# One Trainium2 core: the opening of a three-layer transformer kernel, rearranged

## What is computed

```python
h = jnp.concatenate([meta, x], axis=1)                  # 16 + 256 rows of 2048
xn = h * rsqrt(mean(h * h) + 1e-6) * g_pre_mix
proj = xn @ w_in                                        # the first 512 columns are S5's input u
a_bar = exp(lam * exp(log_dt))                          # 32 groups x 64 complex states
states = associative_scan(a_bar, u @ b_bar)             # s[t] = a_bar * s[t-1] + b_bar u[t]
y = real(c @ states) + d * u
```

## Time and profile before

| | us |
|---|---|
| median of 3 runs | 3298.6 |
| lowest, highest | 3298.03, 3300.4 |
| span of the profiled execution | 3298.9 |
| TensorE busy in it | 3269.3 |
| VectorE, ScalarE, GpSimd busy | 1971.1, 1513.7, 275.8 |

### The profile page before, as it was taken

The page is one execution under the profiler, slowest core; times in us unless marked ns, Lnnn a source line. Parts: engine busy times, 40 slices in busy tenths (PEclk is TensorE's granted clock), DMA queues, the critical chain, the costliest instruction groups (busy, mean ns, idle before and its releaser), DMA issues.

```text
span 3298.9 us, 45001 instructions
## 1 busy us (share of the span) xinstructions
PE 3269.3 (99%) x17255; PEld 2811.2 (85%) x17255; DVE 1971.1 (60%) x2228; ACT 1513.7 (46%) x1754; POOL 275.8 (8%) x238
## 2 busy tenths in 40 slices
PE   8999999999999999999999999999999999999999
PEld 7998888888888888888888888888888888888887
DVE  7888665555555655565555555564656555555565
ACT  5335454344444544545443444454454534444444
POOL 6432000000000034000000000001400000000000
PEclk9999999999999999999999999999999999999999
DMA  7544555655555555455555666655545565666664
GB/s 208 154 129 162 195 192 191 190 186 188 196 194 191 168 183 166 141 179 183 188 189 191 189 193 191 191 176 173 180 146 177 191 192 188 190 190 192 191 192 152
DMA packets 249097, 598.55 MB, mean 181 GB/s; under 512 B 22297, under 2 KB 63993, under 8 KB 247945
## 3 DMA queue, kind: packets, MB, share of 16 engines
q1 hardware_dynamic: 247800, 591.10, 56.2%
q0 software_dynamic: 800, 5.31, 0.4%
q10 hardware_dynamic: 384, 0.58, 0.1%
HBM read 594.86 MB, written 2.10 MB: 181 GB/s over the span
## 4 chain that ended last, share of the span: by engine, by line
PE 95%; DVE 3%; ACT 1%; DVEq 1%; issue 0%; DMA 0%; ACTq 0%; POOLq 0%
PE ps L1023 31%; PE ps L628 21%; PE ps L1281 19%; PE ps L634 11%; PE ps L984 3%; PE ps L706 2%; PE ps L698 2%; PE ps L699 1%; PE ps L571 1%; DVE wlo L2040 1%; PE ps L1171 0%; PE ps L1170 0%; PE ps L580 0%; DVE wlo L2647 0%; PE ps L1205 0%
## 5 line engine op out<-in xcount | busy, mean ns | idle before, releaser
L2040 DVE TENSOR_TENSOR wlo<-raw,whi 128x2048 fp32r<-128x2048 f32 (+1 forms) x425 | 973.6, 2291 | 653.3 <-ACT whi L1397 652.7
L1397 ACT CAST whi<-raw 128x2048 fp32r<-128x2048 f32 (+2 forms) x427 | 809.3, 1895 | 532.1 <-PE ps L634 426.0
L628 PE MATMUL ps<-xT,whi 128*128 128x512 f32 x3072 | 733.5, 391 | 1.4 <-DVE xT L2058 1.1
L1023 PE MATMUL ps<-whi,stage 128*128 128x512 f32 x3040 | 725.9, 389 | 0.0
L1023 PEld LDWEIGHTS ps<-whi,stage 128*128 128x128 f32 x3040 | 570.3, 188 | 118.1
L628 PEld LDWEIGHTS ps<-xT,whi 128*128 128x128 f32 x3072 | 564.6, 188 | 111.6 <-issue 1.3
L1281 PE MATMUL ps<-whi,xT 128*128 128x512 f32 (+1 forms) x1792 | 444.5, 389 | 1.1 <-DVE wlo L2647 0.9
L634 PEld LDWEIGHTS ps<-xT,wlo 128*128 128x128 f32 x3072 | 393.9, 191 | 15.0
L634 PE MATMUL ps<-xT,wlo 128*128 128x256 f32 x3072 | 398.5, 283 | 0.0
L1754 ACT CAST stage<-big 128x256 fp32r (+1 forms) x384 | 137.0, 404 | 546.4 <-PE ps L1023 535.5
L1023 PE MATMUL ps<-wlo,stage 128*128 128x512 f32 x1520 | 381.1, 389 | 0.0
(11 more groups left out here) (424 smaller groups left out, 2332.1 us busy)
## 6 DMA issues: line engine op xcount, KB each, us to landing
raw<-in_mlp_w SPq DMA_DIRECT2D x128, 1024.0 KB, 5.1
raw<-in_w_up SPq DMA_DIRECT2D x128, 1024.0 KB, 5.3
raw<-in_w_down SPq DMA_DIRECT2D x128, 1024.0 KB, 5.5
raw<-in_w_in SPq DMA_DIRECT2D x100, 1024.0 KB, 5.1
raw<-in_w_o SPq DMA_DIRECT2D x32, 1024.0 KB, 5.5
raw<-in_w_out SPq DMA_DIRECT2D x16, 1024.0 KB, 5.0
raw<-in_w_in SPq DMA_DIRECT2D x16, 832.0 KB, 4.4
raw<-in_w_uq SPq DMA_DIRECT2D x4, 1024.0 KB, 5.0
```

The lines of the kernel that those rows point to most:

```text
L628: mm(psum(bank + j), whi[:, u % 2, c:c + P], xT[:, k, :], start=k == 0, stop=False)
L1023: return mm(psum(bank + 2 * r + n), x_of(kk, part, r), w[:, u % 2, c:c + 512], start=begin and kk == part == 0 and w is whi, stop=stop)
L1397: act.copy(whi[:, u % 2, 0:width], raw[:, u, 0:width]).then_inc(sig["hi"], 1)
L2040: tt(wlo[:, u % 2, 0:width], raw[:, u, 0:width], whi[:, u % 2, 0:width].bitcast(F32), SUB).then_inc(sig["lo"], 1)
```

## The change

Four things, all in the first 60 us:

1. *Meta rows over 128 partitions.* Each meta row is loaded as 8 rows of 256 (`xm`, [128, 256]). VectorE squares them, TensorE sums the 8 parts by a mask matrix made from the identity (`meta_mask`), ScalarE and VectorE make the inverse root, GpSimd scales, TensorE turns two blocks, VectorE multiplies by the gains, ScalarE and VectorE write the high and the low part straight into `xT1`. A chain of nine steps on one semaphore, `meta`. The tiles' transposes and evictions have 256 columns now. The products still have 272.
2. *Squares shared, loads moved.* VectorE squares x's first half and half of the second, ScalarE the other half. The constants, the meta rows and the gain `g_pre_mix` are loaded by ScalarE's queue, the other eight small vectors by SP's, ahead of the weights. Fillers: 5, 4 and 5 instead of 12 and 12. The gain has a transpose of its own, early; the other vectors' transpose comes after tile 7.
3. *First panel cast in pieces and used by row tile.* ScalarE casts four pieces of 512, one after every two tiles; TensorE takes both column blocks of a tile as it comes (`both_high`), after tiles 0 to 7.
4. *S5 tables doubled together.* The angle times 16 is wrapped and put through the sines together with the angle (128 x 32 instead of 128 x 16), and both tables grow in one doubling of four rounds with twice the columns. The S5 steps on ScalarE and VectorE stand later: exponential after tile 15, `angles` and `first_power` after the low half of panel 1, the sines after the cast of panel 2, and `tiles(U_STAGE, 0)` behind them.

```diff
 tensor
-            pe.wait_ge(sig["ld_cst"], 16)
-            keep_busy(12, 1)
-            pe.wait_ge(sig["ld_rows"], 16 * N_ROW_LOADS)
-            pe.wait_ge(sig["dtr"], 1)
-            tr(psum(0, P), colrow[0], ident).then_inc(sig["cpy"], 1)
-            keep_busy(12, 1)
...
-                    tr(psum(4 + k % 4, META), xm[:, c], ident[0:META, 0:META])
                     for r in range(RT):
-                        last = tr(psum(4 + k % 4, P, at=META + P * r), x[:, r, c], ident)
+                        last = tr(psum(4 + k % 4, P, at=P * r), x[:, r, c], ident)
...
+            pe.wait_ge(sig["ld_cst"], 16)
+            keep_busy(5, 1)
+            pe.wait_ge(sig["meta"], M_SQUARED)
+            mm(psum(3, 1), meta_mask, ss[:, 2:3], start=True, stop=True).then_inc(sig["meta"], 1)
+            pe.wait_ge(sig["ld_g"], 16)
+            tr(psum(6, KD), colrow[0][0:KD, :], ident[0:KD, 0:KD]).then_inc(sig["gcl"], 1)
+            keep_busy(4, 1)
+            pe.wait_ge(sig["meta"], M_SCALED)
+            for j in range(2):
+                last = tr(psum(2, P, at=P * j), xm[:, P * j:P * j + P], ident)
+            last.then_inc(sig["meta"], 1)
+            keep_busy(5, 1)
+            pe.wait_ge(sig["xna"], 1)
             pe.wait_ge(sig["xn"], norm_at["xn"] + 1)
             rows_in(0, 4)
             pe.wait_ge(sig["xn"], norm_at["xn"] + 2)
             rows_in(4, 8)
-            pe.wait_ge(sig["cols"], 1)
+            pe.wait_ge(sig["ld_rows"], 16 * N_ROW_LOADS)
+            pe.wait_ge(sig["dtr"], 1)
+            tr(psum(3, P, at=SEQ), colrow[0], ident).then_inc(sig["cpy"], 1)
...
+                    def both_high():
+                        pe.wait_ge(sig["meta"], M_LOW)
+                        for k in range(8):
+                            if k < 6:
+                                pe.wait_ge(sig["hi0"], k // 2 + 1)
+                            else:
+                                pe.wait_ge(sig["hi"], 4 * (Q + q) + 1)
+                            pe.wait_ge(sig["xt"], norm_at["xt"] + k + 1)
+                            for j in range(2):
+                                hi = whi[:, 0, k * 256 + j * P:k * 256 + j * P + P]
+                                mm(psum(j, L), hi, xT1[:, k, 0, :], start=k == 0, stop=False)
+                                mm(psum(j, L), hi, xT1[:, k, 1, :], start=False, stop=False)
+                    if first and u == 0:
+                        both_high()
+                        pe.wait_ge(sig["xnp"], 1)
+                        pe.wait_ge(sig["xnh"], 1)
+                        rows_in(8, 12)
+                        low(0)
+                        rows_in(12, KD)
+                        low(1)
+                        continue
+                    if first and u == 1:
+                        high(0)
+                        high(1)
+                        low(0)
+                        low(1)
+                        continue
 scalar
-            fn(big[:, 0:D], x[:, 0, :], ACT.Square, accum_out=ss[:, 0:1])
...
+            act.wait_ge(sig["meta"], M_SUMMED)
+            fn(rs[:, 2:3], psum(3, 1), ACT.Sqrt, scale=1.0 / D, bias=eps).then_inc(sig["meta"], 1)
             act.wait_ge(sig["ld_x1"], 16)
+            fn(big[:, 3072:4096], x[:, 1, 0:1024], ACT.Square, accum_out=ss[:, 3:4])
+            act.wait_ge(sig["xsq"], 1)
+            fn(rs[:, 0:1], ss[:, 0:1], ACT.Sqrt, scale=1.0 / D, bias=eps)
             act.drain()
+            act.wait_ge(sig["xsq"], 2)
+            fn(rs[:, 1:2], ss[:, 3:4], ACT.Sqrt, scale=1.0 / D, bias=ss[:, 1:2]).then_inc(sig["ss"], 1)
+            act.wait_ge(sig["meta"], M_GAINED)
+            fn(xT1[:, :, 0, 0:META], meta_t.rearrange("p (k m) -> p k m", m=META), ACT.Copy).then_inc(sig["meta"], 1)
             act.wait_ge(sig["rsr"], first["rsr"] + 1)
+            fn(x[:, 1, 0:512], x[:, 1, 0:512], ACT.Copy, scale=rs[:, 1:2]).then_inc(sig["xna"], 1)
...
+            act.wait_ge(sig["raw0"], 16 * (Q + 1))
+            for i in range(4):
+                rows_hi(2 * i, 2 * i + 2)
+                c = slice(512 * i, 512 * i + 512)
+                act.copy(whi[:, 0, c], raw[:, 0, c]).then_inc(sig["hi0" if i < 3 else "hi"], 1)
+            rows_hi(8, 12)
+            split(Q, 1, D, used=False)
+            rows_hi(12, KD)
+            act.wait_ge(sig["cols"], 1)
+            fn(prm[:, 0, :], cols[:, V_LOG_DT:V_LOG_DT + ST], ACT.Exp).then_inc(sig["prm_a"], 1)
+            split(Q, 2, D)
+            act.wait_ge(sig["prm_b"], 1)
+            fn(prm[:, 7, :], prm[:, 1, :], ACT.Exp)
+            fn(ang[:, 3, :], ang[:, 1, :], ACT.Sin)
+            fn(ang[:, 4, :], ang[:, 2, :], ACT.Sin).then_inc(sig["prm_a"], 1)
+            tiles(U_STAGE, 0)
+            split(Q, 3, D)
 vector
+            dve.wait_ge(sig["ld_x"], 16)
+            stt(big[:, 0:D], x[:, 0, :], 1.0, x[:, 0, :], MUL, MUL, accum_out=ss[:, 0:1]).then_inc(sig["xsq"], 1)
+            dve.wait_ge(sig["meta"], M_ROOT)
+            dve.reciprocal(rs[:, 2:3], rs[:, 2:3]).then_inc(sig["meta"], 1)
+            dve.wait_ge(sig["ld_x1"], 16)
+            stt(big[:, D:D + 1024], x[:, 1, 1024:D], 1.0, x[:, 1, 1024:D], MUL, MUL, accum_out=ss[:, 1:2])
...
+            dve.wait_ge(sig["meta"], M_TURNED)
+            dve.drain()
+            tt(meta_t.rearrange("p (b j m) -> p b j m", b=8, j=2), psum(2, META_COLS).rearrange("p (j m b) -> p b j m", j=2, m=META),
+               cols[:, 0:KD].rearrange("p (b j) -> p b j", j=2).unsqueeze(3).to_broadcast([P, 8, 2, META]), MUL)\
+                .then_inc(sig["meta"], 1)
...
+            dve.wait_ge(sig["meta"], M_HIGH)
+            tt(xT1[:, :, 1, 0:META], meta_t.rearrange("p (k m) -> p k m", m=META), xT1[:, :, 0, 0:META].bitcast(F32), SUB)\
+                .then_inc(sig["meta"], 1)
...
-            angles()
             rows_lo(4, 8)
-            quad(Q, D, {1: lambda: (first_power(), rows_lo(8, KD)), 3: powers, 4: b_blocks})
+            dve.wait_ge(sig["cpy"], 1)
+            copy(cols[:, KD:P], psum(3, P - KD, at=SEQ + KD)).then_inc(sig["cols"], 1)
+            quad(Q, D, {1: lambda: rows_lo(8, KD), 2: lambda: (angles(), first_power()), 3: powers, 4: b_blocks})
 gpsimd
-                    doubled(fine_c, fine_s, 0)
-                    pool.drain()
-                    pool.tensor_copy(coarse_c[:, :, 1:2], fine_c[:, :, FINE - 1:FINE])
-                    pool.tensor_copy(coarse_s[:, :, 1:2], fine_s[:, :, FINE - 1:FINE])
-                    doubled(coarse_c, coarse_s, 1)
+                    c, s = [t.rearrange("p j (t k) -> p j t k", t=2) for t in (table_c, table_s)]
+                    for to, turn in ((c, 4), (s, 3)):
+                        pool.tensor_copy(to[:, :, :, 0], ang[:, turn, :].rearrange("p (t j) -> p j t", t=2))
+                    n = 1
+                    while n < FINE:
+                        cn, sn = [t[:, :, :, n - 1:n].to_broadcast([P, ST, 2, n]) for t in (c, s)]
+                        d = [v[:, :, :, 0:n] for v in dbl]
+                        pool.drain()
+                        tt(d[0], c[:, :, :, 0:n], cn, MUL)
+                        tt(d[1], s[:, :, :, 0:n], sn, MUL)
+                        tt(d[2], s[:, :, :, 0:n], cn, MUL)
+                        tt(d[3], c[:, :, :, 0:n], sn, MUL)
+                        pool.drain()
+                        tt(c[:, :, :, n:2 * n], d[0], d[1], SUB)
+                        tt(s[:, :, :, n:2 * n], d[2], d[3], ADD)
+                        n *= 2
```

160 lines of the change are left out of this document (65 added, 95 removed).

## The result

The changed kernel takes 3308.9 us (median of 13 runs, 3305.6 to 3309.6); the kernel before, run beside it, 3300.1 (13 runs, 3298.0 to 3301.6). The ratio is 1.0025, 95% interval 1.0017 to 1.0032. That is slower by 0.25%, clear of no change; the interval reaches to both sides of the 0.2% that the prediction set as its bound. 3297.8 and a range up to 3302.0 were predicted. The prediction started from 3298.6, the median of 3 runs; with 13 runs the kernel before takes 3300.1, so 1.5 us of the distance between 3297.8 and 3308.9 are not the change's. The profiled execution took 3309.45 us with a span of 3307.7.

A forecast was written before the change was run, and what follows sets the result against it. TensorE was taken as the bound, its opening counting only as far as the S5 chain came earlier. Low half 2.4 us earlier less 1.6 for the clock made 0.8: 3298.6 - 0.8 = 3297.8 us, range 3293.6 to 3302.0.

The forecast's parts named there:

- What bounds it: Whole opening: TensorE is busy 3269.3 of 3298.9 us; an earlier opening counts only as far as the S5 chain is earlier.
- Start of the transposes: Opening: TensorE's transposes start at 13.9 instead of 16.28, 2.4 us gained, with the meta chain hidden in the wait for x.
- Rows and the first panel: TensorE's first panels: the first ends at 27.1 instead of 32.9, the second at 33.1 instead of 38.87; 5.8 us ahead.
- The S5 parameters: ScalarE and VectorE: GpSimd starts at 35.5, 8.9 us later; TensorE waits 2.4 us for copies, keeping 3.3 of its lead.
- The tables: GpSimd's S5 tables: one doubling replaces two; ready at 52.0 against 51.73, the first rotation 8.5 us later at 60.4.
- rival (c): GpSimd's tables: four-dimensional operands cost twice per column, rounds 18.5 instead of 10.5 us, total 3306.3; chance 0.06.
- What arrives: VectorE uses the rotation at 60.5, low half 2.4 us earlier; TensorE waits 2.6, clock loses 1.6; net 0.8 won.
- (a): Cold opening: fewer fillers let transposes and the 32 matmuls run at half speed, 2.5 us later, total 3300.2; chance 0.32.
- (d): First panel's load waits some 3 us behind the eight small transfers, ScalarE's first tile too, total 3300.8; chance 0.07.
- (b): TensorE's lead arrives: cheaper tables, rotation out at 57.5, the 3.3 lead and 1.7 wait come through, total 3293.6; chance 0.13.

The follow-up runs named there:

- Experiment 5: Changed kernel with opening fillers of 10 and 8 instead of the first 5 and 4, in TensorE's idle time: 3307.8 us.
- experiment 1: Changed kernel with the meta rows' transfer moved from second on ScalarE's queue to the head of SP's queue: 3303.0 us.
- experiment 6: Changed kernel with VectorE squaring x's first half before it waits for the meta rows, transfers left in place: 3307.2 us.
- experiment 7: Kernel before with only the S5 tables doubled together, all steps in their old places: 3302.35 us.
- experiment 10: Changed kernel with meta rows first on SP's queue, S5 steps earlier, and 18 filler matmuls in TensorE's wait for a low half: 3299.5 us.
- experiment 3: The version with both edits: changed kernel with meta rows first on SP's queue and S5 steps earlier on ScalarE and VectorE: 3296.6 us.
- experiment 2: Changed kernel with the S5 parameter steps put earlier on ScalarE and VectorE, meta rows as late as ever: 3300.7 us.

## Why the prediction was wrong, step by step

*What bounds it.* Right: an earlier opening counted only as far as the S5 chain was earlier. Experiment 5 shows it: there TensorE reached its wait 3.7 us earlier, and 2.6 of these were waited away.

*Start of the transposes.* The first step that failed, and the larger: "The meta chain itself (sum, root, inverse, scaling, turning) runs in the wait for x and costs nothing while the constants land by 8". The constants landed at 6.2. The condition left out the meta rows' own landing, which had no row and no bound: issued behind the constants and beside 2 MB of x they took 9.1 us to 10.26, and VectorE's list has them ahead of x's squares. The inverse came at 16.1, and the transposes at 17.6, not 13.9. Of this, the landing is worth 3.65 us (experiment 1), the order alone 0.8 (experiment 6). With the meta rows there in time the rest of this part was right: in experiment 1 the transposes start at 13.65.

*Rows and the first panel.* From the first transpose to the panel's end it took 13.6 us, 13.2 were predicted; the part was right but for its start, even with a cold stretch. The second panel ended at 37.6, predicted 33.1.

*The S5 parameters.* The mechanism and the sum were right: from the end of the angles' predecessors to GpSimd's start 4.8 us where 4.8 were predicted (30.7 to 35.5; 35.1 to 39.9), ScalarE's copies in the way with 2.2 us of TensorE's time (2.4 predicted). All of it stood 4.4 us later than predicted, because the opening did. The prediction gave this wait no price in clock; 6 x 0.28 = 1.7 us of TensorE's time went there, and TensorE, predicted 3.3 us ahead of before at its next wait, came to it at 71.99, 2.6 behind before.

*The tables.* 17.2 us where 16.5 were predicted, and 0.64 us for a 256 wide instruction, as interpolated: no slow operands, rival (c)'s mechanism was not there. But its condition was, "once the tables end after 54; then each us counts": they ended at 57.1, from a late start. The outcome, 3306.3 there, was nearest to what came; the cause was not the one named.

*What arrives.* The second step that failed: "The first rotation follows 8.5 later" and "The next low half, without a GpSimd instruction in its way". The rotation took 10.4 us: one of its steps was stopped by a low half of VectorE's (L3021 took 2.99 us; in experiment 6 that one took 1.12 and L3017 3.22). The following low half had GpSimd's next rotation beside it and took 3.41, not 2.28. TensorE's wait was 4.3 (2.6 predicted), and the clock behind it cost 2.6 (1.6 predicted): from the end of that low half to the next use of a rotation it took 21.4 us (76.22 to 97.61), 18.8 before (71.04 to 89.82).

The terms add up: start 4.4, tables 0.7, rotation 1.9, from its use to the low half's end 0.6, clock 1.0 make 8.6 us, and the third use is 7.8 later where 0.8 earlier was predicted.

Experiment 1 tells the two steps apart, since it gives the prediction the opening that it assumed. Its tables run from 34.86 to 52.80 (35.5 to 52.0 predicted), and still the rotation is used at 62.91 and not at 60.5, the low half ends at 71.58 and not at 68.6, TensorE waits 6.8 us and not 2.6, and the clock costs 2.6: the median is 3303.0, 2.8 above before where 0.8 below was predicted. So even without the late meta rows the forecast gain would not have come.

*The rivals.* (a) occurred in part (the first panel's products were cold until 24.0 and warm behind it), and was worth about 1.1 and not 2.5. (d) did not: the first panel landed at 13.6. (b) did not.

So two things, each of which costs by itself: the opening late by the meta rows, and S5 steps without reserve. With the early places the late meta rows cost 4.1 us of median (3300.7 against 3296.6), with the late places 5.9. The late places cost 6.4 with early meta rows (3303.0 against 3296.6), 8.2 with late ones. The prediction had seen the late places and priced their start rightly; what it missed is that nothing behind them had room for it.

On queues: the constants had landed at 6.2. The Trainium skill, DMA: Bandwidth & Descriptors, Specifications, gives a first-byte latency of about 1 us from GpSimd and 0.6 from ScalarE, and the prediction's estimate from it was 7.4. That difference of 0.4 us is small beside what the traffic did: in the version with both edits the same transfer on the same queue took 2.8 us, not 5.4. On ports: VectorE's pair of two-input instructions took 2.68 us beside GpSimd and 0.85 without, and one GpSimd instruction of a rotation 2.99 against 1.12. The Trainium skill, SBUF — State Buffer, Who interferes with whom, has the two engines contend for a shared pair of ports, by an exclusive lock, when VectorE reads two inputs from SBUF and GpSimd reads SBUF too; these rows agree. That "fewer, longer GpSimd instructions only shift who waits" is seen in experiment 7 only in so far as the wait shifts: the same rotation, come 9.5 us earlier, makes `b_blocks` 9.0 us long instead of 3.8.

**Open.** Parts 1 to 3 of the change were not run without part 4, so what the pieces of the first panel are worth alone is not shown. The meta rows were moved to another queue and to its head at once, so which of the two made them early is not shown either. Nor is it shown why a wait lowers the clock in one kernel and a like one not in another.

## What to carry to other kernels

For each step that is moved or newly put in an engine's list, bound the landing of every transfer that the list waits for, not only of the one that was the issue: the place in the list makes a small late transfer hold up all that stands behind it. When work is taken off the bound engine's opening, move the side chain that it will meet forward by as much, or the lead becomes a wait and the wait a lower clock. A repair should be tried on the version that already has the others, as its worth there can be smaller (4.1 against 5.9 us for the meta rows here), and a filler worth 1.7 us can't be told from a clock that falls at another place.

## What the runs showed of the hardware that was not expected

- A small transfer beside large ones took its time more by its place among them than by its size: 128 KB took 9.1 us on ScalarE's queue beside x on SP's, and 2.4 at the head of SP's queue, ahead of x. The 64.5 KB constants, on ScalarE's queue in both, took 5.4 and 2.8. From the version with both edits:

```profile
big<-in_meta_tokens SPq DMA_DIRECT2D x1, 128.0 KB, 2.4
...
cst<-in_constants ACTq DMA_DIRECT2D x1, 64.5 KB, 2.8
```

- The length of a wait did not decide by itself whether the clock fell. It fell behind a wait of 1.26 us (experiment 10), and stayed at 1.00 behind 1.04 at the same place (experiment 3). Behind 2.2 us for ScalarE's copies it was 0.72 from 40 to 46 in the changed kernel and 1.00 in experiments 5 and 6. Behind 2.8 us for the same low half it stayed at 1.00 in experiment 2 and was 0.72 from 66 to 72 in experiment 3. TensorE's wait and a window behind it, experiment 2, then the wait in experiment 3:

```profile
PE ps L734 <- DVE wlo L2086: 3.6, 2, 2.8
...
70.00:72.00 2.00, 1.82 (x14) 1.00 0.30 53
```

```profile
66.83 2.07 PE L736 MATMUL ps<-xT,wlo 128*128 128x272 f32 x8 [2.80 <-DVE wlo L2087]
```

- GpSimd's product of 128 x 256, four-dimensional and with a broadcast operand, takes 0.64 us: with 0.42 at 128 and 1.12 at 544 columns that is a line with some 0.2 at none.
